# A hybrid decoder step: dense matmuls dealt anew among the norms and the query tiles, two weight loads ahead of the cache loads, evictions within the rotary embedding

## The reference, cut to what matters

```python
h = rmsnorm(x, norm_g); proj = h @ w_in        # about 8000 columns, split among the mixers
out_lru = (rg_lru(causal_conv(lru_x)) * silu(lru_z)) @ w_lru_out
q, k = rope(rmsnorm(q)), rope(rmsnorm(k))       # sparse attention: pooled blocks, selected
out_nsa = (attention(q, k, v, cache) * silu(nsa_z)) @ w_nsa_out    # blocks and a window
out_dn = (rmsnorm(gated_delta(l2norm(q), l2norm(k), v)) * silu(dn_z)) @ w_dn_out
x = x + (sum of sigmoid(merge gate) * branch) @ w_out
```

## Time and profile before

| | us |
|---|---|
| median of 3 runs | 2047.75 |
| lowest, highest | 2038.22, 2049.31 |
| profiled execution | 2039.3 |
| its span, first to last instruction | 2037.5 |

### The profile page before, as it was taken

How to read it: one execution, slowest core, us unless ns; L and a number is a source line. 1 busy time by engine, 2 the same in 40 slices (tenths; PEclk the granted TensorE clock), 3 DMA queues, 4 the chain that set the end, 5 groups by cost and what they waited for, 6 DMA issues and landing times.

```text
span 2037.5 us, 29510 instructions
## 1 busy us (share of the span) xinstructions
PE 1914.2 (94%) x11822; PEld 1380.1 (68%) x11822; DVE 750.2 (37%) x1838; ACT 520.8 (26%) x1161; POOL 88.2 (4%) x132
## 2 busy tenths in 40 slices
PE   6999999999499899999999999999994998999999
PEld 5777788885365377777467777888763644777763
DVE  2548243313425534311125563332232454433110
ACT  3143212113136612100112332121140475211000
POOL 0000201010110000000000010010110100000000
PEclk9999999989799899999999999999997999999999
DMA  6213111101431035435032132011115110553401
GB/s 228 88 62 96 54 41 24 63 27 63 125 107 32 11 91 177 138 104 172 0 149 83 45 106 63 22 38 53 37 61 166 52 32 11 153 175 107 164 28 46
DMA packets 183007, 167.75 MB, mean 82 GB/s; under 512 B 48656, under 2 KB 174018, under 8 KB 182294
## 3 DMA queue, kind: packets, MB, share of 16 engines
q1 hardware_dynamic: 178644, 147.79, 24.0%
q0 software_dynamic: 4064, 18.03, 2.4%
q10 hardware_dynamic: 162, 0.05, 0.0%
HBM read 151.34 MB, written 21.71 MB: 85 GB/s over the span
## 4 chain that ended last, share of the span: by engine, by line
PE 88%; DVE 3%; SPq 3%; issue 3%; ACT 2%; DMA 1%; ACTq 0%; DVEq 0%
PE PS L835 61%; PE PS L775 5%; PE PS L1206 2%; SPq L585 1%; PE PS L1037 1%; PE PS L1219 1%; PE PS L1055 1%; PE PS L1057 1%; PE PS L1275 1%; PE PS L1126 1%; PE PS L941 1%; PE PS L1285 1%; PE PS L1360 1%; PE PS L1148 1%; DVE PS L2109 1%
## 5 line engine op out<-in xcount | busy, mean ns | idle before, releaser
L835 PE MATMUL PS<-hT,ring 128*128 128x288 f32 x3968 | 1056.7, 413 | 51.9 <-DMA ring<-in_w_in 34.8
L835 PEld LDWEIGHTS PS<-hT,ring 128*128 128x128 f32 x3968 | 734.0, 191 | 267.9 <-issue 58.3
L835 PE MATMUL PS<-zs,owr 128*128 128x288 f32 x768 | 210.2, 415 | 20.7 <-DVE arena L1801 20.7
L835 PEld LDWEIGHTS PS<-zs,owr 128*128 128x128 f32 x768 | 145.8, 193 | 65.8 <-DVE arena L1801 21.6
L775 PE MATMUL PS<-con,arena 128*128 128x128 f32 (+5 forms) x934 | 146.1, 283 | 16.4 <-DMA arena<-in_nsa_k_norm 10.5
L775 PEld LDWEIGHTS PS<-con,arena 128*128 128x128 f32 (+5 forms) x934 | 109.2, 142 | 76.4 <-issue 44.2
L1463 ACT ACTIVATE sg<-PS 128x288 f32<-128x288 f32 x96 | 38.8, 404 | 352.3 <-PE PS L835 352.2
L835 PE MATMUL PS<-arena 128*128 128x512 f32 (+1 forms) x320 | 124.8, 593 | 2.1 <-issue 2.1
L1805 DVE SCALAR_TENSOR_TENSOR mpr<-sg,PS 128x288 f32<-128x288 f32 x64 | 29.1, 454 | 208.7 <-PE PS L835 206.0
L1765 DVE SCALAR_TENSOR_TENSOR arena<-arena,par 128x512 f32<-128x512 f32 x192 | 99.5, 518 | 6.8
L835 PEld LDWEIGHTS PS<-arena 128*128 128x128 f32 (+1 forms) x320 | 52.7, 179 | 71.1 <-issue 70.9
(11 more groups left out here) (284 smaller groups left out, 1727.1 us busy)
## 6 DMA issues: line engine op xcount, KB each, us to landing
ring<-in_w_in SPq DMA_DIRECT2D x54, 1024.0 KB, 5.3
arena<-in_cache_nsa_kv SPq DMA_DIRECT2D x128, 192.0 KB, 2.6
ring<-in_w_in SPq DMA_DIRECT2D x32, 256.0 KB, 3.7
arena<-in_state_nsa_win SPq DMA_DIRECT2D x32, 256.0 KB, 3.2
arena<-in_cache_nsa_kv SPq DMA_DIRECT2D x128, 64.0 KB, 1.8
arena<-in_w_out SPq DMA_DIRECT2D x4, 2048.0 KB, 9.4
out_win_sample<-in_state_nsa_win POOLq DMA_DIRECT2D x2, 4032.0 KB, 22.4
arena<-in_x_prompt SPq DMA_DIRECT2D x8, 512.0 KB, 8.4
```

The costliest lines, as they stand in the source:

```text
L835: ins = mm(to, w, x, start=start, stop=stop, skip_group_check=True)
```

## The change

`late(total, slot)` takes the place of `spread` in the attention: the steps of a pair of slots go by a weight of 2 for query tile 0, 3, 4 and 5 for tiles 1, 2 and 3, and 5 for the slots behind them. The calls of `fill` in both norms, before the wait for K and between the transposition groups are made smaller. In SP's order slot 21 and the third output weights come before the wait for `st_ok` and the cache loads. ACT no longer takes the units issued before the last broadcast ahead of the SiLUs, only those up to `U_MG0`; DVE takes units between the steps of the rotary embedding. At the start tile 2 has a semaphore of its own, tile 3 and the sample rows share `x_in3`, and ACT and DVE take tiles 0 and 1 first.

```diff
--- before.py
+++ after.py
@@ -244,6 +244,13 @@
     return {"lx": C_LX, "lz": C_LZ, "dc": C_DQKV, "dz": C_DZ, "kv": C_KV, "mg": C_MG}[kind] + c * P
 
 
+def late(total, slot):
+
+    weight = [2 + min(k, N_UNIT - 1) // 16 for k in range(0, N_SLOT, 2)]
+    upto = [total * sum(weight[:k]) // sum(weight) for k in range(len(weight) + 1)]
+    return upto[slot // 2 + 1] - upto[slot // 2]
+
+
 def spread(total, n, i):
 
     return total * (i + 1) // n - total * i // n
@@ -272,7 +279,7 @@
 LO_OUT = 16 * 6
 
 LAYER_SEMS = """
-x_in0 x_in1 x_in2 par_in lrow_in w_in0 w_in1 ow_in0 ow_in1 par_t ssq_ok x_ps rt_ok rr_ok xn_ok x_t sq_ok ms_ok rstd_ok h_ok pj pa pv lam_ok lh_t u_ok lgp
+x_in0 x_in1 x_in2 x_in3 par_in lrow_in w_in0 w_in1 ow_in0 ow_in1 par_t ssq_ok x_ps rt_ok rr_ok xn_ok x_t sq_ok ms_ok rstd_ok h_ok pj pa pv lam_ok lh_t u_ok lgp
 lg at_ok lt_ok lq_ok lru_ok lc_ok lc_in lo_t lo_ok gt_t gt_ok gs_ok bc_ok nk_sw nq_sw qk_ok kt_t kt_e vc_mm
 c_ok c_s c_m c_e c_t c_c c_pv c_n a_s a_m a_p a_r a_n a_t a_ca a_cd a_v z_o
 qb_ok ck_in wk_in cv_in s_pl s_pe s_kt s_ke s_t s_ed s_ea s_sg s_sc s_pv s_cm s_ce
@@ -281,7 +288,7 @@
 i_wm i_x i_xm f_mm f_u f_v f_w m_mm u_mm f_m q_w q_s q_n q_oe b_gl b_pe b_so b_vt
 b_vn b_vm b_sn dn_ok mg_ok v_chain a_chain small_in sm_in ln_ok xr_in xs_out wo_in st_ok kvo_ok
 """.split()
-WHOLE = "x_in0 x_in1 x_in2 w_in0 w_in1 ow_in0 ow_in1 pj pa pv xr_in xs_out v_chain a_chain"
+WHOLE = "x_in0 x_in1 x_in2 x_in3 w_in0 w_in1 ow_in0 ow_in1 pj pa pv xr_in xs_out v_chain a_chain"
 PER_LAYER = dict(
     par_in=192, lrow_in=48, par_t=1, ssq_ok=1, x_ps=1, rt_ok=5, rr_ok=5, xn_ok=5, x_t=9, sq_ok=19, ms_ok=5, rstd_ok=5,
     h_ok=9, lam_ok=1, lh_t=1, u_ok=4, lgp=8, lg=8, at_ok=1, lt_ok=1, lq_ok=1, lru_ok=1, lc_ok=1, lc_in=1, lo_t=2,
@@ -507,10 +514,10 @@
         def _(sp):
             sp.dma_start(con[:, 0:NFIRST], dram["con"][:, 0:NFIRST]).then_inc(s["con_id"], 16)
             for k in range(4):
-                sp.dma_start(xr[k], dram["x_prompt"][0, k * P:(k + 1) * P, :]).then_inc(s[f"x_in{min(k, 2)}"], 16)
+                sp.dma_start(xr[k], dram["x_prompt"][0, k * P:(k + 1) * P, :]).then_inc(s[f"x_in{k}"], 16)
             x_s = dram["x_sample"].rearrange("b t c -> (b t) c")
             for f in range(2):
-                sp.dma_start(xr[4][f * T_S:(f + 1) * T_S], x_s[:, f * 512:(f + 1) * 512]).then_inc(s["x_in2"], 16)
+                sp.dma_start(xr[4][f * T_S:(f + 1) * T_S], x_s[:, f * 512:(f + 1) * 512]).then_inc(s["x_in3"], 16)
 
             def small_weights(l):
                 w_in = at_layer("w_in", l).rearrange("a (j p) c -> p (a j) c", p=P)
@@ -615,13 +622,15 @@
                 out_weights(l * NO + 1)
                 weights(l * NS + 19)
                 weights(l * NS + 20)
+                weights(l * NS + 21)
+                out_weights(l * NO + 2)
                 sp.wait_ge(s["st_ok"], past["st_ok"] + 1)
                 sp.wait_ge(s["dn_ok"], past["dn_ok"] + 1)
                 cached_keys(0)
                 window_keys(0)
                 cached_values(0)
                 window_values(0)
-                for g in (21, 22, 23, 24):
+                for g in (22, 23, 24):
                     weights(l * NS + g)
                     out_weights(l * NO + g - 19)
                 sp.wait_ge(s["a_p"], past["a_p"] + N_UNIT)
@@ -959,16 +968,16 @@
                 ins.then_inc(s["lo_t"], 1)
 
                 pe.wait_ge(s["lo_ok"], past["lo_ok"] + 3)
-                fill(8, u0 + U_MG0)
+                fill(4, u0 + U_MG0)
                 square_sums(past, "dn", "sum", dsq[:, 0:4])
-                fill(8, u0 + U_MG0)
+                fill(4, u0 + U_MG0)
                 square_sums(past, "dn_k", "sum", dsq[:, 4:8])
-                fill(12, u0 + U_MG0)
+                fill(6, u0 + U_MG0)
                 for norm, n in (("dn", 0), ("dn_k", 4)):
                     for h in range(2):
-                        fill(5, u0 + U_MG0)
+                        fill(3, u0 + U_MG0)
                         broadcast(past, norm, dsq[:, n], h)
-                fill(8, u0 + U_MG0)
+                fill(4, u0 + U_MG0)
                 pe.wait_ge(s["bm_ok"], past["bm_ok"] + 4)
                 pe.wait_ge(s["gb_ok"], past["gb_ok"] + 1)
                 n_iw = n_ix = 0
@@ -1152,21 +1161,21 @@
                             fill(4, u0 + U_MG0)
 
                 pe.wait_ge(s["b_sn"], past["b_sn"] + DN_H)
+                fill(2, u0 + U_MG2)
+                square_sums(past, "o", "sum", dc[:, 4:8])
+                fill(4, u0 + U_MG2)
+                square_sums(past, "k", "sum2", rs7[:, 4:7])
                 fill(6, u0 + U_MG2)
-                square_sums(past, "o", "sum", dc[:, 4:8])
+                square_sums(past, "q", "sum2", rs7[:, 0:4])
                 fill(8, u0 + U_MG2)
-                square_sums(past, "k", "sum2", rs7[:, 4:7])
-                fill(8, u0 + U_MG2)
-                square_sums(past, "q", "sum2", rs7[:, 0:4])
-                fill(12, u0 + U_MG2)
                 for norm, roots in (("o", dc[:, 4]), ("k", rs7[:, 4]), ("q", rs7[:, 0])):
                     for h in range(2):
-                        fill(5, u0 + U_MG2)
+                        fill(3, u0 + U_MG2)
                         broadcast(past, norm, roots, h)
                 dense_to(u0 + U_MG0)
                 pe.wait_ge(s["bm_ok"], past["bm_ok"] + 10)
 
-                fill(32, u0 + U_MG2)
+                fill(16, u0 + U_MG2)
                 pe.wait_ge(s["qk_ok"], past["qk_ok"] + 1)
                 for k, (t, n) in enumerate(TILES):
                     if k >= 2:
@@ -1178,7 +1187,7 @@
                         ins = turn(flat[0:n, c * P:(c + 1) * P], src)
                     step("kt_t")
                     ins.then_inc(s["kt_t"], 1)
-                    fill(6, u0 + U_MG2)
+                    fill(4, u0 + U_MG2)
 
                 pe.wait_ge(s["kt_e"], past["kt_e"] + NTILE)
                 for k in range(4):
@@ -1195,7 +1204,7 @@
 
                 for slot in range(N_SLOT):
                     if slot % 2 == 0:
-                        fill(spread(120, (N_SLOT + 1) // 2, slot // 2), u0 + U_MG2)
+                        fill(late(120, slot), u0 + U_MG2)
                     if slot < N_UNIT and slot % 2 == 0:
                         if slot:
                             pe.wait_ge(s["a_p"], past["a_p"] + slot)
@@ -1399,7 +1408,7 @@
                 past = so_far(l)
                 for k in tiles:
                     if l == 0:
-                        act.wait_ge(s[f"x_in{min(k, 2)}"], 16 if k < 2 else 64)
+                        act.wait_ge(s[f"x_in{min(k, 3)}"], 16 if k < 3 else 48)
                     else:
                         act.wait_ge(s["pv"], taken((l - 1) * N_ALL + U_WO + 2 * k + (2 if k < 4 else 1), "V"))
                     link(A(dump[:, 0:xr[k].shape[1]], xr[k], ACT.Square, accum_out=ssq[:, k:k + 1]))
@@ -1418,7 +1427,8 @@
             parameter_rows(act, 0)
             act.wait_ge(s["con_id"], 16)
             link(A(dump[:, 0:1], C("eps"), ACT.Sqrt))
-            rows_scaled(0, (0, 1, 2))
+            rows_scaled(0, (0, 1))
+            rows_scaled(0, (2,))
             rows_scaled(0, (3,))
             rows_scaled(0, (4,))
             for l in range(DEPTH):
@@ -1595,7 +1605,6 @@
                 root_of("o", dc[:, 4])
                 root_of("k", rs7[:, 4])
                 root_of("q", rs7[:, 0])
-                take_before("bc_ok", 10)
                 take_to(u0 + U_MG0)
                 act.wait_ge(s["pa"], taken(u0 + U_MG0, "A"))
                 A(zs[:, 8:12], zs[:, 8:12], ACT.Silu).then_inc(s["silu_ok"], 1)
@@ -1730,11 +1739,13 @@
                             PS[:, 2, :].rearrange("p (c f t) -> p c f t", c=4, f=2),
                             gains.rearrange("p (f c) -> p c f", f=2).unsqueeze(3).to_broadcast([P, 4, 2, n])).then_inc(s["h_ok"], 1)
 
-            for k in range(3):
-                row_root(0, k)
+            row_root(0, 0)
+            row_root(0, 1)
             parameters(0)
-            for k in range(3):
-                turned_rows(0, k)
+            turned_rows(0, 0)
+            row_root(0, 2)
+            turned_rows(0, 1)
+            turned_rows(0, 2)
             row_root(0, 3)
             for l in range(DEPTH):
                 past = so_far(l)
@@ -2041,7 +2052,6 @@
                     ins.then_inc(s["bm_ok"], 1)
                 for h in range(2):
                     times_roots("q", h, qk7[:, 0:4], prm("qn")).then_inc(s["bm_ok"], 1)
-                take_to(u0 + U_MG0)
                 dve.wait_ge(s["bm_ok"], past["bm_ok"] + 10)
                 dve.wait_ge(s["silu_ok"], past["silu_ok"] + 4)
                 mul(zs[:, 8:12], zs[:, 8:12], dc[:, 0:4]).then_inc(s["dn_ok"], 1)
@@ -2049,8 +2059,14 @@
                     dve.wait_ge(s[landed_rows], past[landed_rows] + 64)
                     x, y = qk7[:, n:m], rs7[:, n:m]
                     link(mul(y, y, rep(C("sin"), m - n)))
+                    if n == 0:
```

(5 more changed lines are left out.)

## The result

The changed kernel takes 1953.2 us (median of 4 runs, 1951.9 to 1954.6), the kernel before took 2048.5 beside it. The ratio is 0.9545 with a 95% interval of 0.9515 to 0.9576: faster, by 4.6%. The forecast was 1960 in a range of 1942 to 1994. The profiled execution has a span of 1950.1 us against 2037.5.

The account below looks back on a forecast made before the run. TensorE was taken as the bound, busy 1914 of 2037.5 us. Layers -40.6 and -40.4 and start -3.0 sum to -84.0 from 2039.3: 1955.3, raised for the median to 1960 us, range 1942 to 1994.

Parts of the forecast that it names:

- first norms, three turns: In the first norms, three broadcast turns lose up to 0.5 us each: +1.0 us per layer (0 to 1.5).
- first merge unit behind the SiLUs: In the second norms, PE waits for a bank that ACT evicts after both SiLUs: +1.9 us per layer (0 to 4).
- middle stretch, idle: From the last norm product to the attention, PE's idle 27.3 and 28.7 us become 4.0 in each layer.
- middle stretch, clock: Between the last norm product and the attention, the 4.1 us per layer lost at low clock goes.
- window keys behind a slot: At the sample stage, the second sequence's keys load after a 1 MB slot and output weights: +1.0 us per layer (0 to 5).
- attention, idle: In the prompt attention, PE's idle 13.7 and 15.6 us become 4.5 in each layer (2 to 9).
- attention, clock: In the prompt attention, the low clock's loss of 4.7 us in layer 0 and 1.2 in layer 1 goes.
- start: At the kernel's start, PE's wait for ACT to scale the first rows goes: -3.0 us (0 to -4).
- the norms' thin cover: In the norms, 1 to 2 us gaps and a gap before K give back 12 us a layer: 1984 us; chance 0.13.
- the unfilled attention: In the attention, steps miss the gaps or evictions lengthen the chain, 26.2 us less gain: 1986 us; chance 0.10.
- the late slots: In query tile 1 or 3, weight slots come late again behind SP's waits: 2040 us; chance 0.03.
- The slower one, by clock: In the middle stretch and tiles 0 and 1, thinned work runs at 1.2 GHz: +76 us a layer, 2112 us; chance 0.02.

Follow-up runs that it names:

- the repetition: The changed kernel run again unaltered on another chip: 1950.3 us, ratio 0.9549 to the kernel before.
- the one with five gaps closed: Changed kernel with DVE emptying the bank ahead of K, even dealing, and steps moved ahead of three waits (norm product, copied rows, tile 2's output): 1926.8 us.

## Why the prediction was right

The sum was 84.0 us and the two profiled executions differ by 87.4. By its steps:

| step, both layers | forecast | measured |
|---|---|---|
| first norms, three turns | +2.0 | 0: no gap there |
| wait for the last state | -2.8 | -2.8 |
| Tanh among the logarithms | -3.6 | -3.5 |
| first merge unit behind the SiLUs | +3.8 | +0.5 |
| middle stretch, idle | -48.0 | 27.3 and 28.7 to 4.3 and 4.0: -47.7 |
| middle stretch, clock | -8.2 | -5.3: 2.9 us left in layer 0 |
| window keys behind a slot | +2.0 | 0 |
| attention, idle | -20.3 | 13.7 and 15.6 to 4.9 and 4.5: -19.9 |
| attention, clock | -5.9 | -4.7 in layer 0, none in layer 1, where tile 1 now loses 1.7 |
| start | -3.0 | first dense matmul 3.7 earlier (20.68 to 16.97) |

The large idle terms held within half a microsecond. The middle one did so because it was a count of steps against the lengths of DVE's instructions: PE waits 3.69 us for the bank, where the sum had 4.0. The attention's idle time rested in part on round guesses of 1.5 us for each of three places, and that their sum held is partly luck. So is the small distance of 3.4 us as a whole: three small terms and the start were sized about 8 us too high, and the two clock terms some 4 us too good.

*First norms.* Three steps and the broadcast's own 0.7 us stand beside DVE's 1.35 us, and DVE's 0.45 us for a bank fell where it did no harm: PE is busy 112.97 of 113 us from 203 on.

*The SiLUs.* The step gave the first merge unit 1.9 us a layer, without saying when ACT begins the SiLUs, so what was too long in it can't be redone. Timeline of ScalarE in the changed kernel's second norms:

```profile
470.31 1.83 ACT L1493 ACTIVATE arena<-arena 128x576 f32<-128x576 f32 x3
472.04 0.39 ACT L1468 ACTIVATE zs<-PS 128x288 f32<-128x288 f32 x1
472.45 1.28 ACT L1610 ACT_TABLE_LOAD   x1
473.74 2.12 ACT L1610 ACTIVATE zs<-zs 128x2304 f32<-128x2304 f32 x1
475.77 2.11 ACT L1611 ACTIVATE zs<-zs 128x2304 f32<-128x2304 f32 x1
477.79 0.39 ACT L1473 ACTIVATE sg<-PS 128x288 f32<-128x288 f32 x1
```

There is one load, ahead of the SiLUs: Tanh follows SiLU with none, while from Tanh to SiLU the kernel before had one (at 509.73). PE waits 0.25 us for this unit, not 1.9. The Trainium skill (ScalarE: Activation LUTs, What ACT_TABLE_LOAD costs) gives a switch 1.38 us of drain beside its 1.28 us load. These rows agree with the load and have no room for the drain: the load at 472.45 ends at 473.73 and SiLU starts at 473.74.

*The window keys.* SP issues them at 671.61, right behind a slot at 669.26 and output weights at 671.20, as the step said, and the sample stage starts at 671.10. PE shows no wait for them, so the price was 0, the lower bound. The first cache loads begin 23.1 us behind the start of the DeltaNet's product instead of 4.0, 19 us later where I had said 15; that cost nothing either.

*The clock* is the one place where a reason fell. I wrote that a gap of 4 us did not stand before any slow stretch. Behind 3.69 us twelve records took 6.1 us in layer 0 and 3.3 in layer 1 of the same execution, and in the repetition it was the other way round (3.3 and 5.1). After such a gap it can go either way, and a forecast should carry both. The rows that I had could have warned me: behind the 1.39 us wait of the earlier trace rows twelve records took 4.59 us, where twelve take 3.18 at full clock. And one of my own signs of being wrong did show: the clock in tiles 0 and 1 was to stay at 1.0, and in layer 1 it left it for a part of 8 us, which cost 1.7 us.

Three more points. A step of 0.49 us does not follow from 16 records in 4.15 us, which divide to 0.52; it is the distance from the start of one such group to what comes right behind it, 3.9 us for 16 records. My addition of 4 us for the median took the kernel before's distance between profile and median to stay; it shrank to 1.3 us with the gaps. And I credited the weight wait to SP's order in the text of the step while naming the later demand too; the runs show that either is enough, so as a cause I had one too many.

Of the rivals, the norms' thin cover, the unfilled attention and the late slots did not come about. The slower one, by clock, did so only for the 1.7 us above, but the run with no steps in tiles 0 and 1 shows that it was the right thing to fear.

## What to carry to other kernels

Where one engine is busy nearly throughout, write the ledger of its gaps and give each gap the dense work that fits, counted in steps of one matmul: dense work should lie where the chain is long, and a fill call belongs ahead of a wait, not behind it, wherever the banks allow. When two edits remove the same wait, try each alone; one may be free to drop. And thin stretches can cost twice, by their gaps and by the lower clock of what stands between them (18 and 22 us in the run with no steps in two tiles).

## What the runs showed of the hardware

In the run with no steps in tiles 0 and 1 the mean clock of TensorE was 0.64 over 32 us in which PE was busy 25.4 us and no gap was longer than 2.5 us, and 0.65 in layer 1. The Trainium skill (TensorE: Matmul & The Clock Gate, HAM oscillation — how this bites in real kernels) gives as its abstract rule that PE must have no idle gap beyond a certain length, and every gap here is shorter than that. The clock fell all the same, as it had in the kernel before over 8 us, and the measurement decides. A single gap of 3.69 us lowered the clock in one layer and not in the other of the same run.

The largest loss of clock that is left has no gap at all in the trace. Near the end of the DeltaNet part PE does products of 16 columns each (64 records) with no dense step between them. In the changed kernel, layer 0:

```profile
422.65 9.20 PE L1135 MATMUL PS<-arena 128*128 128x16 f32 x64
431.69 4.19 PE L844 MATMUL PS<-hT,ring 128*128 128x288 f32 x8
```
```profile
424.00:440.00 16.00, 16.00 (x80) 13.70 (x80) 1.10 (x2) 0.41 (x1) 7.51 (x4) 0.68 0.00 0
```

PE is busy for all of the 16 us, and its mean clock is 0.68, so part of the stretch ran at 1.2 GHz; eight dense records took 4.19 us instead of 2.2. That is 5.1 us lost, and as much in layer 1. The kernel before has the same place, and so has the one with five gaps closed, where the clock is 0.68 over such 16 us in both layers. I overlooked it: the edits of this change do not reach it, and whether dense steps among these products would cure it was not tried.

One program's times spread less with the gaps closed: 5 us in the changed kernel (1949.2 to 1954.0), 0.9 us in the run with five edits. Which of the five did it was not separated.
